# A two-layer hybrid attention encoder: its grouped attention written as 24 equal steps, the differential products scaled by GpSimd, one filler weight chunk converted a step sooner

## The chip, the cores and the metric

The kernel runs on one core of a Trainium2 chip. The metric is the device time of one execution in microseconds (us); the time before is 1885.14 us, the median of three runs (1883.15 to 1885.39).

## What is computed

Two sequences (256 and 512 tokens of width 1024) go through two layers and a final norm. A layer, from the reference:

```python
q_g, k_g, v_g, q_d, k_d, v_d = jnp.split(rms_norm(x) @ w_in, SPLITS, axis=-1)
o_g = softmax(q_g @ k_g.T * scale) @ v_g                                   # 8 heads of 64, 2 key/value heads
o_d = rms_norm((softmax(q1 @ k1.T) - lam * softmax(q2 @ k2.T)) @ v_d)      # 4 heads, values of 128
x = x + concat([o_g, o_d]) @ w_out
x = x + (silu(gate) * up) @ w_down
```

(These lines are the reference's, shortened.) Attention is over the whole sequence, without a mask. All arithmetic is 32-bit; the kernel splits each matmul operand into a rounded high part and a low part and adds three products (`mm3`, line 1676).

## The kernel before

Tokens stand in six tiles of 128 rows: t = 0, 1 belong to the short sequence ("prompt" tiles below, 256 keys) and t = 2 to 5 to the long one ("sample" tiles, 512 keys). A layer is the input projections, then attention, then the output projection and the feed-forward part. Only attention is touched. It has eight *pairs* p of two heads; p = 0 to 3 are grouped attention, p = 4 to 7 differential attention (one pair is one differential head with its two maps). Pair and tile give the step e = 6p + t, from 0 to 47; GROUPED is 24.

Each engine has its own instruction list, and the order of the work is that of these lists, written out by hand; semaphores (`Signal`) couple them. There is no planner. The work of a grouped step:

- TensorE (PE): `scores` of a head (three matmuls of 64 rows into one PSUM bank; four banks, 2·(t mod 2) + h), `transpose_prob` of its exponentials (2 or 4 blocks of 128), `product` with the values (10 or 20 matmuls of 64 columns).
- VectorE (DVE): `row_max` of a head's scores (line 1342), the low part of the transposed probabilities (`probT_low`, line 1368), reciprocals (`inverse_sums`, line 1349), `take_product` (line 1388), which scales the product into the `mix` tile.
- ScalarE (ACT): `exp` (line 925), the high part of the transposed probabilities (`probT_high`, line 946).

When the tiles of a pair are done, their `mix` blocks are transposed in two parts (t = 0, 1 and t = 2 to 5; `transpose_mix`, line 1746), and ACT and DVE split the result (`mixT_high`, line 940; `mixT_low`, line 1376). Once in a pair ACT and GpSimd (POOL) split the next pair's queries and keys (`split_high`, line 934; `split_low`, line 655), in a prompt and a sample part.

The grouped pair before (three functions `gqa_pair`, lines 955, 1401 and 1792) is not the same in all its six steps. TensorE asks for the scores of t = 3 with the two heads one behind the other, and so for those of t = 2; for t = 4, 5, 0 and 1 it puts a transpose or a product between the heads:

```python
scores(l, e0 + (T + 1), 1, 0)          # end of a pair, lines 1818 to 1823
gqa_product(l, p, t, 0, vcol)
scores(l, e0 + (T + 1), 1, 1)
gqa_product(l, p, t, 1, vcol)
scores(l, e0 + (T + 2), 2, 0, p * 2 + 3)
scores(l, e0 + (T + 2), 2, 1)
```

ScalarE's exponentials run up to two steps ahead. In pairs 1 and 2 one 128x1024 weight chunk of the output projection is converted at t = 3 (`high_at`, line 732, on ACT, and `low`, line 1119, on DVE).

The differential step (`diff_step`, lines 988, 1431 and 1861) has on TensorE: scores of both heads of step e + 2, a `fill` (six 128x512 matmuls of the output projection for pairs 0 to 3, line 1839), the transposes of the combined map, and the product of step e - 1. ScalarE reads each product twice from PSUM: `squares` (line 975) for its norm, and, after GpSimd has worked out the inverse root (`head_rms`, line 664), `normed` (line 982), which scales the product into `mix`. TensorE's next product waits for `normed` (signal `mix_diff`, line 1835). The fills need four chunks; the third and fourth are converted by ACT at the end of step 35 and by DVE at the ends of steps 35 and 36. In pair 7 ACT and DVE also convert four 128x512 operands (`output_high`, line 739; `operand_low`, line 1166). A mix transpose of a differential pair waits also for the low part of the step before, because it borrows that bank (line 1752). The first fill (e = 24) waits for the mix of pair 3 (line 1849), every later one for `add_fill` of the one before (lines 1476 and 1847).

## Time and profile before

| | |
|---|---|
| median of three runs | 1885.14 us |
| the profiled execution | 1883.45 us |
| its span, first to last instruction | 1881.6 us |
| TensorE busy, share of the span | 1788.8 us, 95% |
| VectorE busy | 1186.2 us, 63% |
| ScalarE busy | 824.1 us, 44% |
| GpSimd busy | 208.4 us, 11% |
| mean granted TensorE clock | 0.994 |
| differential stage of layer 0 | 285.7 to 384.3 us |

All steps below are made against the profiled execution; what it has outside its span is 1.85 us. The two layers run alike: in layer 1 the grouped and the differential stage stand about 925 us later. Matmuls are pipelined: the profile's end of one lies behind the start of the next, so the time that a matmul costs is read from start to start.

### The profile page before, as it was taken

Reading aid. Unit: us, or ns where it says so; the run is one execution under the profiler, and the core shown is the slowest. Engines: PE = TensorE matmul, PEld = TensorE weight load, DVE = VectorE, ACT = ScalarE, POOL = GpSimd, SP = SyncE. Lnnn points to the kernel's source line nnn. Section 1 sums busy time; section 2 is a strip of 40 time slices with the busy share of each in tenths; the row PEclk is TensorE's granted clock in tenths of the full one; section 3 lists DMA queues with packets and bytes.
Section 4 is the critical chain, followed back from the end, with each engine's and each line's share of the span. In section 5 each row is a group of like instructions: output and inputs, shape, how many; then the busy total and the mean of one; then the engine's idle time right before and its main releaser. Section 6 shows DMA issues by size and latency. Waiting matters only on the chain.

```text
span 1881.6 us, 28640 instructions
## 1 busy us (share of the span) xinstructions
PE 1788.8 (95%) x11280; PEld 1565.5 (83%) x11280; DVE 1186.2 (63%) x2055; ACT 824.1 (44%) x1807; POOL 208.4 (11%) x311
## 2 busy tenths in 40 slices
PE   5999899898999999999999999999989999999998
PEld 5888677677999999999888877677779898989896
DVE  4655777866656565656565467776757565756564
ACT  3323777744343433333332347676443342424242
POOL 2301123222000000000012011232400000000000
PEclk9999999999999999999999999999999999999999
DMA  4221000111231312121221110002022222222222
GB/s 155 68 68 45 13 13 1 36 56 56 68 90 46 90 45 90 45 90 45 68 68 57 56 34 13 13 24 68 1 79 68 68 68 68 68 68 68 68 74 84
DMA packets 121908, 108.20 MB, mean 58 GB/s; under 512 B 3472, under 2 KB 95760, under 8 KB 121776
## 3 DMA queue, kind: packets, MB, share of 16 engines
q1 hardware_dynamic: 120096, 100.74, 18.0%
q0 software_dynamic: 960, 3.28, 0.5%
q8 instruction: 90, 1.47, 0.3%
q10 hardware_dynamic: 720, 2.36, 0.3%
q14 instruction: 42, 0.34, 0.1%
HBM read 103.22 MB, written 3.15 MB: 57 GB/s over the span
## 4 chain that ended last, share of the span: by engine, by line
PE 83%; DVE 7%; ACT 6%; issue 2%; POOL 1%; DMA 1%; SPq 0%; POOLq 0%; ACTq 0%; DVEq 0%
PE bank L1678 15%; PE bank L1680 13%; PE bank L1679 13%; PE bank L2018 11%; PE bank L2022 11%; PE bank L2020 11%; PE bank L1768 3%; PE bank L1759 2%; ACT stage L931 2%; DVE neg_max L1346 1%; ACT stage L951 1%; DVE stage L1372 1%; PE bank L1937 1%; PE bank L1719 1%; POOL hrstd L607 1%
## 5 line engine op out<-in xcount | busy, mean ns | idle before, releaser
L1678 PE MATMUL bank<-w_hi,hT_hi 128*128 128x512 f32 (+1 forms) x624 | 244.7, 392 | 10.8 <-DVE w_lo L1121 4.6
L1680 PE MATMUL bank<-w_hi,hT_lo 128*128 128x512 f32 (+1 forms) x624 | 234.1, 375 | 0.0
L1679 PE MATMUL bank<-w_lo,hT_hi 128*128 128x512 f32 (+1 forms) x624 | 233.6, 374 | 0.0
L1242 DVE TENSOR_TENSOR x<-x,bank 128x512 f32<-128x512 f32 x120 | 81.2, 686 | 119.5 <-PE bank L1680 119.0
L1678 PEld LDWEIGHTS bank<-w_hi,hT_hi 128*128 128x128 f32 x624 | 117.9, 189 | 41.0 <-issue 8.5
L2018 PE MATMUL bank<-hT_hi,w_hi 128*128 128x384 f32 x368 | 125.3, 340 | 11.3 <-issue 7.4
L1680 PEld LDWEIGHTS bank<-w_hi,hT_lo 128*128 128x128 f32 x624 | 117.8, 189 | 21.6
L1768 PEld LDWEIGHTS bank<-v,stage 128*128 128x128 f16 x2400 | 102.0, 98 | 39.5 <-issue 25.3
L1679 PEld LDWEIGHTS bank<-w_lo,hT_hi 128*128 128x128 f32 x624 | 118.2, 189 | 17.2
L1768 PE MATMUL bank<-v,stage 128*128 128x64 bf16 (+1 forms) x2400 | 116.6, 203 | 13.2 <-DVE stage L1372 11.1
L2022 PE MATMUL bank<-hT_hi,w_lo 128*128 128x384 f32 x368 | 125.1, 340 | 0.0
L605 POOL TENSOR_TENSOR ms<-ss,eps_col 128x1 f32<-128x1 f32 x30 | 6.6, 220 | 1066.9 <-ACT headsq L779 1066.9
L2020 PE MATMUL bank<-hT_lo,w_hi 128*128 128x384 f32 x368 | 124.6, 339 | 0.0
L1121 DVE TENSOR_TENSOR w_lo<-w_raw,w_hi 128x1024 fp32r<-128x1024 f32 x48 | 58.7, 1223 | 103.8 <-ACT w_hi L730 103.6
L931 ACT ACTIVATE stage<-bank,neg_max 128x512 f32<-128x512 f32 (+1 forms) x192 | 117.1, 614 | 16.0 <-DVE neg_max L1346 15.4
L1346 DVE TENSOR_REDUCE neg_max<-bank 128x1 f32<-128x512 f32 (+1 forms) x192 | 111.3, 590 | 10.9 <-PE bank L1680 10.9
L760 ACT ACTIVATE w_hi<-w_raw 128x512 fp32r<-128x512 f32 x112 | 69.3, 624 | 93.9 <-DMA w_raw<-in_w_down_dram 32.9
L1678 PE MATMUL bank<-w_hi,actT_hi 128*128 128x512 f32 x264 | 104.6, 396 | 0.0
L1680 PE MATMUL bank<-w_hi,actT_lo 128*128 128x512 f32 x264 | 104.3, 395 | 0.0
L1679 PE MATMUL bank<-w_lo,actT_hi 128*128 128x512 f32 x264 | 104.2, 395 | 0.0
L730 ACT ACTIVATE w_hi<-w_raw 128x1024 fp32r<-128x1024 f32 x48 | 50.5, 1057 | 109.7 <-PE bank L1680 108.2
L1171 DVE TENSOR_TENSOR w_lo<-w_raw,w_hi 128x512 fp32r<-128x512 f32 x112 | 75.9, 694 | 22.5 <-ACT w_hi L760 22.5
(209 smaller groups left out, 4620.3 us busy)
## 6 DMA issues: line engine op xcount, KB each, us to landing
x_raw<-in_w_gate_up_dram SPq DMA_DIRECT2D x44, 512.0 KB, 5.1
w_raw<-in_w_gate_up_dram SPq DMA_DIRECT2D x44, 512.0 KB, 4.0
w_raw<-in_w_in_dram SPq DMA_DIRECT2D x36, 512.0 KB, 3.7
w_raw<-in_w_down_dram SPq DMA_DIRECT2D x36, 512.0 KB, 3.8
w_raw<-in_w_out_dram SPq DMA_DIRECT2D x16, 512.0 KB, 3.7
x_raw<-in_w_down_dram SPq DMA_DIRECT2D x8, 512.0 KB, 4.1
out_dram<-stage SPq DMA_DIRECT2D x6, 512.0 KB, 2.6
gain<-in_gains_dram POOLq DMA_DIRECT2D x5, 512.0 KB, 4.8
```

The lines of the kernel that those rows point to most:

```text
L760: act.activation(ring_of(r)[0], raw_of(s)[:, off:off + COLS], ACT.Copy).then_inc(ff_hi.sem, 1)
L931: act.activation(prob[:, b, h, 0:S], bank[:, 2 * b + h, 0:S], ACT.Exp, bias=neg_max[:, b, h:h + 1], accum_out=row_sum[:, t, h:h + 1]).then ...
L1171: dve.tensor_tensor(lo, raw_of(s)[:, off:off + COLS], hi.bitcast(F32), ALU.subtract).then_inc(ff_lo.sem, 1)
L1242: dve.tensor_tensor(xs, xs, bank[:, DOWN_BANK[t], :], ALU.add).then_inc(x_added.sem, 1)
L1346: dve.tensor_reduce(neg_max[:, b, h:h + 1], bank[:, 2 * b + h, 0:S], AX.X, ALU.max, negate=True).then_inc(max_done.sem, 1)
L1678: pe.matmul(out, a_hi, b_hi, start=first, stop=False)
L1679: pe.matmul(out, a_hi, b_lo, start=False, stop=False)
L1680: return pe.matmul(out, a_lo, b_hi, start=False, stop=last)
L1768: last = pe.matmul(out, probT[:, b, a, k, :], v[i][:, k0 // P + k, at(vcol, width)], start=(k, a, i) == terms[0], stop=(k, a, i) == terms[-1])
L2018: pe.matmul(o, b_hi[:, cols], a_hi[:, k, :], start=begin, stop=False, skip_group_check=True)
L2020: pe.matmul(o, b_hi[:, cols], a_lo[:, k, :], start=False, stop=False, skip_group_check=True)
L2022: last = pe.matmul(o, b_lo[:, cols], a_hi[:, k, :], start=False, stop=end, skip_group_check=True)
```

## The change

Grouped attention becomes 24 calls of one `grouped_step` on each engine. TensorE asks for the scores of both heads of step e + 2 together, behind the first head's transposes; the product of a step's second head moves into the next step. `row_max` reduces both heads (two PSUM banks) in one instruction, in the differential steps too, and both heads' exponentials wait for that one signal. ScalarE's exponentials are now one step ahead, and the mix parts are transposed at t = 3 of their own pair and t = 1 of the next (for pair 3 at step 24, inside the first differential step). `normed` goes: ScalarE copies the product unscaled into `mix` right behind `squares` (signal `o_taken`), and GpSimd multiplies it there by the inverse root. The third filler chunk is converted by ACT at the end of step 34 and by DVE at the beginning of step 35; the fourth by ACT at the end of step 35, as before, and by DVE at the beginning of step 36. The diff, without declarations of unchanged meaning:

```diff
 def mixed_at(e):
     p, t = divmod(e, 6)
-    return (p, 0) if t == 4 else (p - 1, 1) if t == 2 and p > PAIRS // 2 else None
+    if e < GROUPED:
+        return (p, 0) if t == 3 else (p - 1, 1) if t == 1 and p else None
+    return (PAIRS // 2 - 1, 1) if e == GROUPED else (p, 0) if t == 4 else (p - 1, 1) if t == 2 and p > PAIRS // 2 else None
...
+        o_taken = Signal("o_taken", 4 * T, credit=1)
+        mix_diff = Signal("mix_diff", 4 * T)
...
                 c = slice(t, t + 1)
                 inverse_rms(l, (p - 4) * T + t, oss[:, c], oss_done, oms[:, c], oms_done, orstd[:, c], orstd_done,
                             eps_row[:, c])
+                pool.wait_ge(orstd_done.sem, orstd_done.at(l, (p - 4) * T + t))
+                pool.wait_ge(o_taken.sem, o_taken.at(l, (p - 4) * T + t))
+                pool.tensor_scalar(mix[:, t, :], mix[:, t, :], orstd[:, c], None, ALU.mult).then_inc(mix_diff.sem, 1)
...
-                act.wait_ge(max_done.sem, max_done.at(l, e * 2 + h))
+                act.wait_ge(max_done.sem, max_done.at(l, e))
                 act.activation(prob[:, b, h, 0:S], bank[:, 2 * b + h, 0:S], ACT.Exp, bias=neg_max[:, b, h:h + 1],
                                accum_out=row_sum[:, t, h:h + 1]).then_inc(exp_done.sem, 1)
...
-            def gqa_pair(l, p, following):
-                e0 = p * T
-                for t in range(T):
-                    probT_high(l, e0 + t, t, 0, 0, P_SCALE)
-                    if t:
-                        exp(l, e0 + (t + 1), (t + 1) % T, 1)
-                    probT_high(l, e0 + t, t, 1, 1, P_SCALE)
-                    exp(l, e0 + (t + 2), (t + 2) % T, 0)
-                    if t == 2:
-                        mixT_high(l, p, 0, True)
-                    if t in (2, 4):
-                        split_high(t // 2 - 1, q_hi, following[0])
-                        split_high(t // 2 - 1, k_hi, following[1])
-                    if t == 3 and p in (1, 2):
-                        high_at(l, CHUNKS_IN + p - 1)
-                exp(l, e0 + (T + 1), 1, 1)
-                mixT_high(l, p, 1, True)
+            def grouped_step(l, e):
+                p, t = divmod(e, T)
+                probT_high(l, e, t, 0, 0, P_SCALE)
+                if mixed_at(e):
+                    mixT_high(l, *mixed_at(e), True)
+                for h in range(2):
+                    exp(l, e + 1, (t + 1) % T, h)
+                probT_high(l, e, t, 1, 1, P_SCALE)
+                if t in (1, 4):
+                    split_high(t // 4, q_hi, p + 1)
+                    split_high(t // 4, k_hi, 8 + (p + 1) // 2 if p < 3 else 10)
+                if t == 3 and p in (1, 2):
+                    high_at(l, CHUNKS_IN + p - 1)
...
-            def normed(l, p, t):
-                act.wait_ge(orstd_done.sem, orstd_done.at(l, (p - 4) * T + t))
-                act.activation(mix[:, t, :], bank[:, BANK_O, 0:P], ACT.Copy,
-                               scale=orstd[:, t:t + 1]).then_inc(mix_diff.sem, 1)
+                act.activation(mix[:, t, :], bank[:, BANK_O, 0:P], ACT.Copy).then_inc(o_taken.sem, 1)
...
-                if e >= GROUPED + 2:
-                    normed(l, *divmod(e - 2, T))
                 if mixed_at(e):
-                    mixT_high(l, *mixed_at(e), False, e)
+                    mixT_high(l, *mixed_at(e), e == GROUPED, e)
...
-                if e == 5 * T + 5:
-                    high_at(l, CHUNKS_IN + 2)
-                    high_at(l, CHUNKS_IN + 3)
+                if e in (5 * T + 4, 5 * T + 5):
+                    high_at(l, CHUNKS_IN + e - 5 * T - 2)
...
+                for h in range(2):
+                    exp(l, 0, 0, h)
+                for e in range(GROUPED):
+                    grouped_step(l, e)
+                for h in range(2):
+                    exp(l, GROUPED + 1, 1, h)
...
-            def row_max(l, e, t, h):
+            def row_max(l, e, t):
                 S = seq_of(t)[1]
                 b = t % 2
-                dve.wait_ge(scores_done.sem, scores_done.at(l, e * 2 + h))
-                dve.tensor_reduce(neg_max[:, b, h:h + 1], bank[:, 2 * b + h, 0:S], AX.X, ALU.max,
+                dve.wait_ge(scores_done.sem, scores_done.at(l, e * 2 + 1))
+                dve.tensor_reduce(neg_max[:, b, :], bank[:, 2 * b:2 * b + 2, 0:S], AX.X, ALU.max,
                                   negate=True).then_inc(max_done.sem, 1)
...
-            def gqa_pair(l, p):
-                e0 = p * T
-                for t in range(T):
-                    if t >= 3:
-                        row_max(l, e0 + (t + 1), (t + 1) % T, 1)
-                    probT_low(l, e0 + t, t, 0, 0, P_SCALE)
-                    inverse_sums(l, e0 + t, t)
-                    if t >= 2 and t < T - 1:
-                        row_max(l, e0 + (t + 2), (t + 2) % T, 0)
-                    if t:
-                        take_product(l, e0 + (t - 1), t - 1)
-                    probT_low(l, e0 + t, t, 1, 1, P_SCALE)
-                    if t == 0:
-                        for h in range(2):
-                            row_max(l, e0 + 3, 3, h)
-                    if t == 2:
-                        mixT_low(l, p, 0, True)
-                    if t == 3 and p in (1, 2):
-                        low(l, CHUNKS_IN + p - 1, CHUNKS_IN + p - 1)
-                for h in range(2):
-                    row_max(l, e0 + (T + 1), 1, h)
-                take_product(l, e0 + (T - 1), T - 1)
-                next_maxima(l, e0 + (T + 2))
-                mixT_low(l, p, 1, True)
+            def grouped_step(l, e):
+                p, t = divmod(e, T)
+                if e:
+                    probT_low(l, e - 1, (t - 1) % T, 1, 1, P_SCALE)
+                probT_low(l, e, t, 0, 0, P_SCALE)
+                if mixed_at(e):
+                    mixT_low(l, *mixed_at(e), True)
+                row_max(l, e + 2, (t + 2) % T)
+                inverse_sums(l, e, t)
+                if e:
+                    take_product(l, e - 1, (t - 1) % T)
+                if t == 3 and p in (1, 2):
+                    low(l, CHUNKS_IN + p - 1, CHUNKS_IN + p - 1)
...
-                ahead = GROUPED < e < STEPS - 2
+                if e in (5 * T + 5, 6 * T):
+                    n = CHUNKS_IN + (2 if e < 6 * T else 3)
+                    low(l, n, n)
                 if combining:
                     inverse_sums(l, e + 1, (t + 1) % T)
-                if ahead:
-                    row_max(l, e + 2, (t + 2) % T, 0)
-                if combining:
                     map_ratio(l, *divmod(e + 1, T))
-                if ahead:
-                    row_max(l, e + 2, (t + 2) % T, 1)
+                if e + 2 < STEPS:
+                    row_max(l, e + 2, (t + 2) % T)
                 if combining:
                     combine(l, *divmod(e + 1, T))
                 if mixed_at(e):
-                    mixT_low(l, *mixed_at(e), False, e)
+                    mixT_low(l, *mixed_at(e), e == GROUPED, e)
                 probT_low(l, e, t, 0, t % 2, map_scale[:, :])
                 if t % 2:
                     add_fill(l, (e - GROUPED) // 2)
-                if e in (5 * T + 5, 6 * T):
-                    n = CHUNKS_IN + (2 if e < 6 * T else 3)
-                    low(l, n, n)
...
+                for e in range(GROUPED):
+                    grouped_step(l, e)
+                probT_low(l, GROUPED - 1, T - 1, 1, 1, P_SCALE)
+                take_product(l, GROUPED - 1, T - 1)
                 second_map_in(l, 4, 0)
...
-            def scores(l, e, t, h, split=None, first=False):
+            def scores(l, e, split=None):
+                t = e % T
                 k0, S, _ = seq_of(t)
                 b = t % 2
                 if split is not None:
                     pe.wait_ge(qk_split.sem, qk_split.at(l, split * 2 + 1))
-                if not first:
-                    pe.wait_ge(exp_done.sem, exp_done.at(l, (e - 2) * 2 + h))
-                rows = slice(h * HD, (h + 1) * HD)
-                mm3(bank[:, 2 * b + h, 0:S], q_hi[rows, t * P:(t + 1) * P], q_lo[rows, t * P:(t + 1) * P],
-                    k_hi[rows, k0:k0 + S], k_lo[rows, k0:k0 + S], True, True).then_inc(scores_done.sem, 1)
+                if e >= 2:
+                    pe.wait_ge(exp_done.sem, exp_done.at(l, (e - 2) * 2 + 1))
+                for h in range(2):
+                    rows = slice(h * HD, (h + 1) * HD)
+                    mm3(bank[:, 2 * b + h, 0:S], q_hi[rows, t * P:(t + 1) * P], q_lo[rows, t * P:(t + 1) * P],
+                        k_hi[rows, k0:k0 + S], k_lo[rows, k0:k0 + S], True, True).then_inc(scores_done.sem, 1)
...
-                e = p * T + t
+            def grouped_product(l, e, h):
+                p, t = divmod(e, T)
                 if h == 0:
                     pe.wait_ge(mix_gqa.sem, mix_gqa.at(l, e - 2))
-                    bank_free_of_mix(l, p, t)
+                    if mixed_at(e):
+                        q, part = mixed_at(e)
+                        pe.wait_ge(mixT_lo_done.sem, mixT_lo_done.at(l, 2 * q + part))
                 pe.wait_ge(pT_lo[h].sem, pT_lo[h].at(l, e))
-                last = product(t, bank[:, BANK_O + t % 2, h * HD:(h + 1) * HD], h, vcol, HD)
+                last = product(t, bank[:, BANK_O + t % 2, h * HD:(h + 1) * HD], h, p // 2 * HD, HD)
                 if h:
                     last.then_inc(o_done.sem, 1)
...
+            def grouped_step(l, e):
+                p, t = divmod(e, T)
                 gqa_transpose(l, e, t, 0)
-                gqa_product(l, p, T - 2, 1, vcol)
+                if mixed_at(e):
+                    transpose_mix(l, *mixed_at(e), True)
+                scores(l, e + 2, {4: p * 2 + 2, 0: p * 2 + 1}.get(t))
+                if e:
+                    grouped_product(l, e - 1, 1)
                 gqa_transpose(l, e, t, 1)
-                scores(l, e0 + (T + 1), 1, 0)
-                gqa_product(l, p, t, 0, vcol)
-                scores(l, e0 + (T + 1), 1, 1)
-                gqa_product(l, p, t, 1, vcol)
-                scores(l, e0 + (T + 2), 2, 0, p * 2 + 3)
-                scores(l, e0 + (T + 2), 2, 1)
-                transpose_mix(l, p, 1, True)
+                grouped_product(l, e, 0)
...
-                pe.wait_ge(mix_diff.sem, mix_diff.at(l, e - GROUPED - 1))
+                pe.wait_ge(o_taken.sem, o_taken.at(l, e - GROUPED - 1))
                 pe.wait_ge(pT_lo[0].sem, pT_lo[0].at(l, e))
                 product(t, bank[:, BANK_O, 0:P], t % 2, (p - 3) * P, P).then_inc(o_done.sem, 1)
...
-                if GROUPED < e < STEPS - 2:
-                    for h in range(2):
-                        scores(l, e + 2, (t + 2) % T, h, {4: p * 2 + 2, 0: p * 2 + 1}.get(t) if h == 0 else None)
+                if e < STEPS - 2:
+                    scores(l, e + 2, {4: p * 2 + 2, 0: p * 2 + 1}.get(t))
                 if mixed_at(e):
-                    transpose_mix(l, *mixed_at(e), False, e)
+                    transpose_mix(l, *mixed_at(e), e == GROUPED, e)
                 fill(l, e - GROUPED)
-                if mixed_at(e - 1):
+                if e > GROUPED and mixed_at(e - 1):
                     q, part = mixed_at(e - 1)
                     pe.wait_ge(mixT_lo_done.sem, mixT_lo_done.at(l, 2 * q + part))
...
+                for t in range(2):
+                    pe.wait_ge(v_rest.sem, v_rest.at(l, T + 2 * t + 1))
+                    scores(l, t, None if t else 0)
+                pe.wait_ge(v_rest.sem, v_rest.at(l, 2 * T - 1))
+                pe.wait_ge(qkT_done.sem, qkT_done.at(l, 4 * T - 1))
+                for e in range(GROUPED):
+                    grouped_step(l, e)
+                grouped_product(l, GROUPED - 1, 1)
```

`grouped_step` calls functions that stand as before (`probT_high`, `exp`, `probT_low`, `inverse_sums`, `take_product`, `gqa_transpose`, `transpose_mix`).

## Rows read from the trace of the kernel before

**Rows 1.** Windows: stretch, length, busy us of PE, PEld, DVE, ACT, POOL, granted clock.
```profile
217.63:240.11 22.48, 20.35 (x284) 15.33 (x283) 17.06 (x40) 16.60 (x43) 3.91 (x4) 1.00 0.08 25
...
285.70:384.28 98.58, 92.08 (x782) 72.72 (x783) 76.11 (x164) 73.60 (x231) 31.19 (x58) 1.00 0.12 33
...
193.30:199.80 6.50, 6.50 (x40) 4.51 (x40) 3.95 (x9) 3.35 (x12) 0.00 (x0) 0.50 0.00 0
```
**Rows 2.** Waits, whole run: engine, line, releaser: us in total, times, longest.
```profile
PE bank L1768 <- DVE stage L1372: 11.1, 24, 0.7
```
**Rows 3.** Timeline of PE, one grouped pair of layer 0: start, us, instruction.
```profile
193.29 1.16 PE L1678 MATMUL bank<-k_hi,q_hi 64*128 64x512 f32 x2 [3.04 <-ACT stage L931]
...
216.24 0.51 PE L1678 MATMUL bank<-k_hi,q_hi 64*128 64x512 f32 x2
...
217.14 0.66 PE L1754 MATMUL bank<-ident,mix 128*128 128x128 f32 x4
217.63 0.60 PE L1759 MATMUL bank<-ident,stage 128*128 128x128 f32 x4
...
223.29 0.47 PE L1768 MATMUL bank<-v,stage 128*128 128x64 bf16 x10
223.59 0.64 PE L1759 MATMUL bank<-ident,stage 128*128 128x128 f32 x4
224.16 0.50 PE L1678 MATMUL bank<-k_hi,q_hi 64*128 64x512 f32 x1
...
225.04 0.76 PE L1768 MATMUL bank<-v,stage 128*128 128x64 bf16 x20
...
230.54 0.38 PE L1678 MATMUL bank<-k_hi,q_hi 64*128 64x256 f32 x1
...
231.09 0.76 PE L1768 MATMUL bank<-v,stage 128*128 128x64 bf16 x20
```
**Rows 4.** Groups by form, 217.63 to 240.11: names, shapes, count, busy us, mean ns, idle.
```profile
L1346 DVE TENSOR_REDUCE neg_max<-bank 128x1 f32<-128x512 f32 x9 | 6.0, 680 | 1.2 <-PE bank L1680 1.2
L1372 DVE SCALAR_TENSOR_TENSOR stage<-bank,stage 128x512 f16<-128x512 f32 x8 | 5.5, 690 | 2.4 <-ACT stage L951 2.1
L931 ACT ACTIVATE stage<-bank,neg_max 128x512 f32<-128x512 f32 x8 | 5.5, 688 | 1.4 <-DVE neg_max L1346 1.4
L951 ACT ACTIVATE stage<-bank 128x512 f16<-128x512 f32 x8 | 4.8, 596 | 0.9 <-PE bank L1759 0.7
...
L1346 DVE TENSOR_REDUCE neg_max<-bank 128x1 f32<-128x256 f32 x4 | 1.7, 414 | 0.2 <-PE bank L1680 0.2
...
L1121 DVE TENSOR_TENSOR w_lo<-w_raw,w_hi 128x1024 fp32r<-128x1024 f32 x1 | 1.2, 1225 | 0.9 <-ACT w_hi L730 0.9
```
**Rows 5.** Timeline of PE where the grouped stage of layer 0 ends.
```profile
283.56 0.66 PE L1754 MATMUL bank<-ident,mix 128*128 128x128 f32 x4
285.73 0.47 PE L1678 MATMUL bank<-w_hi,hT_hi 128*128 128x512 f32 x1 [1.50 <-DVE hT_lo L1382]
```
**Rows 6.** Waits of PE, 285 to 400: line, releaser, us in total, times, longest.
```profile
PE bank L1678 <- DVE w_lo L1121: 2.3, 2, 2.1
PE bank L1754 <- DVE stage L1372: 2.1, 2, 1.5
...
PE bank L1768 <- ACT mix L985: 0.8, 4, 0.2
```
**Rows 7.** Groups by form of GpSimd and one copy, 285.7 to 383, layer 0.
```profile
L985 ACT ACTIVATE mix<-bank,orstd 128x128 f32<-128x128 f32 x23 | 8.5, 368 | 9.5 <-POOL orstd L607 9.1
...
L660 POOL TENSOR_TENSOR k_lo<-qkT,k_hi 128x256 fp32r<-128x256 f32 x3 | 3.7, 1223 | 0.0
...
L660 POOL TENSOR_TENSOR q_lo<-qkT,q_hi 128x256 fp32r<-128x256 f32 x3 | 2.2, 748 | 0.0
```
**Rows 8.** Timeline, all engines, where the differential stage of layer 0 ends.
```profile
385.22 0.55 POOL L607 TENSOR_TENSOR orstd<-oms,neg_half 128x1 f32<-128x1 f32 x1
...
387.16 0.60 PE L1754 MATMUL bank<-ident,mix 128*128 128x128 f32 x4
```

53 lines of the change are left out of this document (4 added, 49 removed).

## The prediction, made before the changed kernel was run

> **What bounds the kernel now.** I read the windows of the attention stage first, then TensorE's waits, then its timeline. TensorE sets the pace: a grouped pair lasts 22.48 us, TensorE is busy for 20.35 of them, VectorE 17.06, ScalarE 16.60; the differential stage has 92.08 busy of 98.58 [rows 1]. What is left between is waiting: products of grouped steps wait for the low part of their probabilities, 24 times, 11.1 us in both layers [rows 2]. The rows to look at are the scores. Where both heads are asked for together, the next work starts 0.90 us later (216.24 to 217.14); where one head stands alone, it takes 0.88 (224.16 to 225.04) [rows 3]. The second head of a pair of calls is thus nearly free, and the old order pays in full for it at t = 4, 5, 0 and 1.
>
> **Scores asked for together.** For a sample tile 2 x 0.88 becomes 0.90: 0.86 saved, twice in a pair. For a prompt tile one head takes 0.55 (230.54 to 231.09) [rows 3]; both together are shown in no row here, so they lie between 0.55 and 1.10; I take 0.57, by the sample row: 0.53 saved, twice in a pair. That is 2.78 a pair and **11.1 us a layer** of TensorE's work; with the prompt tile's upper bound it would be 6.9.
>
> **The waits of the new grouped order.** I worked through the three lists with start-to-start times from the rows: four transposes 0.57, paired scores 0.90, a product of 20 matmuls 0.60 (twice the 0.30 of ten) [rows 3]; high part 0.60, exponential 0.69 (with its accumulator read 0.78 to the end), low part 0.69, each with the next instruction of its engine starting some 0.1 before the end [rows 4]. A sample step is 3.2 us of TensorE, 2.4 of ScalarE and 2.7 of VectorE, so TensorE stays the longest. The maximum over two banks is not in the trace. From 0.41 for 256 columns and 0.68 for 512 the slope gives 1.22 for 1024, and a subtraction of 1024 columns takes 1.225 [rows 4]; the ends are 1.22 and twice 0.68 = 1.36 if it saves nothing, more in a rival below. I take 1.22. In a pair four things end late:
> - t = 1: the mix transposes wait for `take_product` of t = 5, which stands behind a two-bank maximum in VectorE's list: 0.4.
> - t = 2: the low parts of both heads come late because ScalarE does the two prompt splits first: 0.2.
> - t = 3: the mix transposes again, for `take_product` of t = 1: 0.3.
> - t = 5: the first product waits while ScalarE does two sample splits ahead of its high part: 0.5.
>
> Pair 0 lacks the first: 5.2 a layer. In pairs 1 and 2 a chunk is converted at t = 3. Before, a maximum stood behind it on VectorE; now the low part of t = 3's second head does, and TensorE waits for that. From the end of those transposes: high part 0.60, ScalarE's chunk 1.06 (estimate: the 0.60 of 512 columns, doubled, less the fixed share), VectorE's 1.22, low part 0.69, some 0.2 of signals: 3.75, against 1.75 that TensorE has to do (a product, four transposes, prompt scores). It waits 2.0, twice: 4.0 a layer; the ends are 0.5 (the wait that such a place shows now [rows 2]) and 2.0. At the end of the stage the last product has nothing to hide its low part: 0.95. At the seam the first fill starts 2.17 after the mix transposes now, 1.68 beyond their own 0.49 [rows 3, 5]; the new list puts a combine and one-column instructions ahead of `mixT_low`, some 0.9 (estimate from 0.41 for 256 columns, and as much again): 2.6. Sum: 5.2 + 4.0 + 0.95 + 2.6 = **12.75**.
>
> The same measure before: 12 waits of 0.46 [rows 2], each 0.17 longer from start to start (a product at 223.29 with 0.47 on the page is followed at 223.59 [rows 3]), 7.6, and the seam's 1.68: **9.3**. So waits grow by 3.45 and the grouped stage gets 11.1 - 3.45 = **7.65 us a layer** shorter. The stage's start gives nothing: TensorE idles 3.04 us there for exponentials that wait for VectorE's work on the values, and then runs 6.5 us at a granted clock of 0.50, that is 1.2 of 2.4 GHz [rows 1, 3]; the same work is to be done in it.
>
> **The differential steps.** ScalarE's instructions stay as many: a raw copy for a scaled one of the same shape, 0.37 [rows 7]. What goes is its wait for GpSimd, 9.1 us in a stage [rows 7], of which only 0.8 reached TensorE [rows 6]; I count 0.6, since one of the four waits stands just ahead of a longer one. The copy now stands ahead of `output_high` in pair 7, and VectorE waits for that: the two mix waits, 2.1 [rows 6], grow by 0.27 each, with the two-bank order by 0.3: +0.6. GpSimd's scaling, 24 a layer, is not in the trace: between a one-column operation (0.55 [rows 8]) and 256 columns with two inputs (0.75 [rows 7]). I take 0.6. Queued behind it are only the next head's inverse root and the query and key splits, which are read a step or more later; what waits for it, the mix transposes, comes two steps later, and at the stage's end there are 1.39 us between the end of the inverse root and these transposes (385.77 to 387.16 [rows 8]): nothing on the path. If that cover went, 0.6 a layer. The merged maximum lets the first exponential of a step wait 0.54 longer (1.22 against 0.68 [rows 4]); in ScalarE's list it stands behind the high part of the step's map, and that behind a fill on TensorE, so nothing ends later.
>
> Against this stands a rule. GpSimd's split of 256 columns takes 0.75 in one place and 1.22 in another, where VectorE combines maps beside it [rows 7]; the mean shows the slowing, and VectorE's side is small. The Trainium skill (SBUF — State Buffer, "SBUF: two separate sides") makes it an exclusive lock: a GpSimd operation and a VectorE operation with two SBUF inputs block each other for a whole instruction. By that rule every one of the 24 scalings could hold a combine up; it would reach the path at the three places where VectorE ends last, 3 x 0.6 a layer, and the sum would be 3.6 us less gain.
>
> The third chunk: the fill of step 36 waits 2.1 and that of step 37 0.2 for chunks [rows 6]. With the chunk a step earlier, `add_fill` of step 35 ends last in its place: behind the chunk (1.22) VectorE has the maximum, a combine, a low part and that add. Worked through, step 36 still waits 1.2 and step 37 not at all: **1.0 to 1.3 gained**, the ends 0 and 2.3. SP's next chunk load is released by the same conversion, so it comes earlier; that chunk is used only after step 47.
>
> The stage sums to -1.3 - 0.6 + 0.6 = **-1.3 a layer**. Both layers: 2 x (7.65 + 1.3) = 17.9. The profiled execution took 1883.45, the median is 1.69 above it: 1885.1 - 17.9 = **1867**.
>
> **Rivals.**
> - *The clock falls at the new waits.* An idle of 3.04 us was followed by a clock of 0.50 for 6.5 us, one of 2.1 at step 36 by none [rows 1, 3, 6]. The seam's 2.6 lies between them, the chunk waits at 2.0. Each fall costs half of 6.5, 3.25: the seams alone give 1873.5, the four chunk waits as well 1886. The Trainium skill (TensorE: Matmul & The Clock Gate, Part 1) has the same rule, that an idle stretch halves the clock until work has been sustained. Chance 0.13.
> - *The waits are shorter.* If the chunk conversion is hidden as it is now, 1859. Chance 0.1.
> - *Waits take everything back.* With exponentials one step ahead instead of two, each late signal reaches TensorE; a third of a us more in each of the 48 grouped steps would do it: about 1883. For it: every engine has 70% or more to do; against it: the worked lists. Chance 0.06.
> - *The change does not do what it says:* prompt or sample scores do not overlap behind transposes. All 22 us stay unsaved: 1889. The paired calls at 216.24 speak against it. Chance 0.04.
> - *Slower: the two-bank maximum.* If crossing a bank made it cost double, 2.44, VectorE's pair would grow by 4 x 1.22 + 2 x 0.68 = 6.2 to 23.3, above the old 22.48, and the differential stage's 72.72 by over 20 to some 95 of 98.6, with in-order waits on top: some 8 us a layer, 1900. It decides from about 1.9 us on. No instruction of before reads two banks, so only the slope speaks against it. Chance 0.07.
>
> **The numbers.** The forecast has 0.6 and a range of its own of 1861 to 1873 (prompt pairing, chunk, seam). For 8 in 10 the range takes in the shorter waits and the clock at the seams: 1857 to 1877. A measurement of this kernel tells some 0.2% from no change, 3.8 us. Faster by more: 0.6 + 0.1 + 0.11 of the clock case + 0.03 of full waits = 0.84; within: 0.08; slower: 0.08.
>
> **What would show it.** Both heads' score matmuls merged at every step, a pair without a chunk at 18 to 19 us and one with a chunk at 20 to 20.5; `row_max` at 1.2 us; the wait before products at t = 4 of pairs 1 and 2 at 2 us; the seam above 2 us; no PE wait for `mix` on ScalarE; the chunk wait at step 36 replaced by one for `add_fill`. Pairs above 21 us, maxima above 1.4 us or a granted clock below 1 after the start would make it wrong.

## The result, and the profile after

The changed kernel takes **1867.01 us** (median of 4 runs, 1862.12 to 1870.84) where the kernel before takes 1885.27 (4 runs beside it): ratio 0.9901, 95% interval 0.9879 to 0.9923, that is 18.3 us faster with some 4 us of uncertainty. The forecast was 1867, 17.9 faster. The sum came out; this section and the next show that not all of its terms did.

The profiled execution took 1870.84 us, the slowest of the four, with a mean granted clock of 0.987 (before: 0.994). Windows of it: stretch, length, busy time of PE, PEld, DVE, ACT, POOL, granted clock, and last the DMA share and GB/s. The first is the start of grouped attention, the second and third are pairs 1 and 2, each from the second block of transposes of its step t = 1 to that of the next pair's, and the last three are stretches right behind a wait.

```profile
193.06:199.80 6.74, 6.74 (x50) 4.47 (x51) 3.66 (x7) 3.82 (x14) 0.00 (x0) 0.51 0.00 0
214.71:234.66 19.95, 17.51 (x288) 13.50 (x285) 16.29 (x34) 16.35 (x44) 3.94 (x4) 1.00 0.10 28
234.66:255.76 21.10, 18.92 (x288) 15.08 (x285) 16.42 (x34) 16.55 (x44) 3.95 (x4) 0.92 0.08 26
247.38:251.00 3.62, 3.62 (x48) 3.55 (x48) 2.20 (x5) 1.43 (x3) 0.23 (x1) 0.53 0.43 149
276.78:280.50 3.72, 3.72 (x15) 2.25 (x15) 0.48 (x1) 1.49 (x4) 0.00 (x0) 0.68 0.00 0
365.99:369.50 3.51, 3.42 (x11) 2.57 (x12) 2.59 (x6) 1.51 (x7) 1.64 (x3) 0.62 0.14 27
```

A pair that lasted 22.48 [rows 1] lasts 19.95. Pair 2 does the same work in 21.10: in it a stretch runs at 0.53 of the clock. The start is as it was [rows 1].

The timeline of PE, at a prompt tile's scores, pair 0's t = 5, pair 1 from t = 1 to t = 4, the two chunk waits, the seam (the end of the grouped stage), and three waits of the differential stage (start, duration, instruction, idle time before and its releaser):

```profile
206.82 0.39 PE L1652 MATMUL bank<-k_hi,q_hi 64*128 64x256 f32 x2
...
207.38 0.29 PE L1744 MATMUL bank<-v,stage 128*128 128x64 bf16 x4
...
210.74 0.63 PE L1735 MATMUL bank<-ident,stage 128*128 128x128 f32 x4
211.75 0.74 PE L1744 MATMUL bank<-v,stage 128*128 128x64 bf16 x20 [0.37 <-DVE stage L1364]
...
215.27 0.66 PE L1730 MATMUL bank<-ident,mix 128*128 128x128 f32 x4
...
218.24 0.51 PE L1652 MATMUL bank<-k_hi,q_hi 64*128 64x512 f32 x2
...
219.14 0.32 PE L1744 MATMUL bank<-v,stage 128*128 128x64 bf16 x5
...
219.45 0.64 PE L1735 MATMUL bank<-ident,stage 128*128 128x128 f32 x4
220.14 0.74 PE L1744 MATMUL bank<-v,stage 128*128 128x64 bf16 x20
220.72 0.63 PE L1735 MATMUL bank<-ident,stage 128*128 128x128 f32 x4
221.44 0.44 PE L1730 MATMUL bank<-ident,mix 128*128 128x128 f32 x2
...
223.31 0.63 PE L1735 MATMUL bank<-ident,stage 128*128 128x128 f32 x4
223.78 0.75 PE L1744 MATMUL bank<-v,stage 128*128 128x64 bf16 x20
...
227.44 0.76 PE L1744 MATMUL bank<-v,stage 128*128 128x64 bf16 x20 [1.89 <-DVE stage L1364]
...
247.38 1.25 PE L1744 MATMUL bank<-v,stage 128*128 128x64 bf16 x20 [1.89 <-DVE stage L1364]
...
272.25 0.76 PE L1744 MATMUL bank<-v,stage 128*128 128x64 bf16 x20 [0.62 <-DVE stage L1364]
...
273.84 0.65 PE L1730 MATMUL bank<-ident,mix 128*128 128x128 f32 x4
276.78 0.47 PE L1652 MATMUL bank<-w_hi,hT_hi 128*128 128x512 f32 x1 [2.29 <-DVE hT_lo L1374]
...
324.53 0.47 PE L1652 MATMUL bank<-w_hi,hT_hi 128*128 128x512 f32 x1 [1.28 <-DVE x L1453]
...
332.25 0.63 PE L1730 MATMUL bank<-ident,mix 128*128 128x128 f32 x4 [0.59 <-DVE stage L1364]
...
365.99 0.41 PE L1730 MATMUL bank<-ident,mix 128*128 128x128 f32 x2 [2.30 <-DVE stage L1364]
```

Both heads' scores are merged (x2) at every step and cost 0.56 (206.82 to 207.38) and 0.90 (218.24 to 219.14) together; a single head cost 0.55 and 0.88 [rows 3]. From the first work after the start's wait to the first fill it is 83.72 us (193.06 to 276.78), before 92.44 (193.29 to 285.73, [rows 3, 5]): the grouped stage is **8.7 us** shorter in this execution, and 9.0 in the other layer (1111.07 to 1194.52, before 1118.24 to 1210.64).

The waits of PE from 185 to 400 us (engine, line, releaser: us in total, times, longest):

```profile
PE bank L1744 <- DVE stage L1364: 5.4, 6, 1.9
PE bank L1730 <- DVE stage L1364: 3.8, 3, 2.3
...
PE bank L1652 <- DVE hT_lo L1374: 2.3, 1, 2.3
```

Grouped products wait six times, 5.4 us (before, 24 times 11.1 in both layers, 5.55 a layer [rows 2]). No wait for ScalarE's copy is left (0.8 before [rows 6]), and the filler waits for the sum into x (1.28 at 324.53) where it waited 2.1 for `w_lo` [rows 6]. But the mix transposes of the differential stage wait 3.8 where they waited 2.1 [rows 6].

Groups of the differential stage, 276.78 to 375 (names, shapes, count, busy, mean ns, idle):

```profile
L1338 DVE TENSOR_REDUCE neg_max<-bank 128x2 f32<-128x1024 f32 x15 | 18.2, 1217 | 0.0
L672 POOL TENSOR_SCALAR mix<-mix,orstd 128x128 f32<-128x128 f32 x22 | 16.2, 735 | 2.2
```

The maximum over two banks takes 1.22 us. GpSimd's scaling takes 0.74 in the mean. The raw copy takes 0.28 (shown in run 7); the scaled one took 0.37 [rows 7].

### The profile page after: what moved, and what is told of

Read it like the earlier page. It is cut to its first block, busy times and chain, and to the rows that moved or that the text cites. A ratio compares the mean times of both kernels' runs of the same rounds, so it can differ in the third digit from the quotient of the medians.

```text
span 1868.8 us, 28636 instructions
## 1 busy us (share of the span) xinstructions
PE 1776.8 (95%) x11280; PEld 1560.3 (83%) x11280; DVE 1181.0 (63%) x1959; ACT 815.9 (44%) x1807; POOL 240.4 (13%) x359
## 4 chain that ended last, share of the span: by engine, by line
PE 80%; DVE 10%; ACT 6%; issue 2%; DMA 1%; POOL 1%; SPq 0%; POOLq 0%; ACTq 0%; DVEq 0%
PE bank L1652 14%; PE bank L1654 13%; PE bank L1653 13%; PE bank L1968 11%; PE bank L1972 11%; PE bank L1970 11%; DVE neg_max L1338 2%; ACT stage L937 2%; PE bank L1744 2%; PE bank L1735 2%; ACT stage L957 1%; DVE stage L1364 1%; PE bank L1887 1%; PE bank L1693 1%; DVE w_lo L1113 1%
## 5 line engine op out<-in xcount | busy, mean ns | idle before, releaser
L1744 PEld LDWEIGHTS bank<-v,stage 128*128 128x128 f16 x2400 | 106.5, 100 | 29.8 <-DVE stage L1364 13.5
L1338 DVE TENSOR_REDUCE neg_max<-bank 128x2 f32<-128x1024 f32 (+1 forms) x96 | 99.5, 1038 | 3.1 <-PE bank L1654 2.4
L1735 PE MATMUL bank<-ident,stage 128*128 128x128 f32 x480 | 83.6, 291 | 6.6 <-ACT stage L937 6.6
```

Source lines behind the costliest of these rows:

```text
L1338: dve.tensor_reduce(neg_max[:, b, :], bank[:, 2 * b:2 * b + 2, 0:S], AX.X, ALU.max, negate=True).then_inc(max_done.sem, 1)
L1735: last = pe.transpose(bank[:, BANK_PT + b, k * P:(k + 1) * P], prob[:, t % 2, h, k * P:(k + 1) * P], ident[:, :])
L1744: last = pe.matmul(out, probT[:, b, a, k, :], v[i][:, k0 // P + k, at(vcol, width)], start=(k, a, i) == terms[0], stop=(k, a, i) == terms[-1])
```

## The experiments

Each was timed beside the kernel before; I compare ratios to it. Each ratio has an interval of plus or minus 0.13 to 0.25%, 2.5 to 4.6 us, and the difference of two of them is less certain than either, by some 4 to 5 us. Of smaller differences only the traces speak. `e_same`, the changed kernel once more, gives the yardstick.

> The changed kernel once more, unchanged, to have it on the same chip as the two beside it and to see how far its runs differ with the granted clock: 1867 by both theories, between 1862 and 1871, the lower ones with the higher mean clock.

Measured: 1865.1 us (4 runs, 1864.42 to 1867.32), ratio 0.9902 (0.9886 to 0.9918), as in the first timing. Its profiled run had a clock of 0.989 and took 1867.32; of the first timing's runs the fastest, 1862.12, had 0.994. The spread of the changed kernel goes with the clock.

**1. The scores of the two heads apart.**

```diff
-                scores(l, e + 2, ...)
-                if e:
-                    grouped_product(l, e - 1, 1)
+                for h in range(2):
+                    head_scores(l, e + 2, h, ...)
+                    if h == 0 and e:
+                        grouped_product(l, e - 1, 1)
```

> The changed kernel with the scores of the two heads pulled apart again on TensorE: head 0's three matmuls, the product of the step before, then head 1's three. Nothing else moves. Theory (TensorE's own work sets the length of a grouped step): a sample step's scores take 0.88 + 0.88 us instead of 0.90 and a prompt step's 0.55 + 0.55 instead of 0.56, so 2.8 to 4.5 us a pair, 11 to 14 a layer with the last steps' unmoved, 22 to 28 us in all: 1889 to 1895. Rival (the steps wait for VectorE and ScalarE, the pairing is hidden in their round): head 1's scores come later by one product (0.75 us), so the maximum does too, but TensorE's time falls into waits that are there anyway: under 8 us in all. A second rival: the longer matmul time closes the short waits, the clock stays up, and the cost is between the two, 10 to 18.

Measured: 1916.68 us, ratio 1.0168 (1.0145 to 1.0191): **49.7 us** more than the changed kernel, by far the largest effect. It is more than the whole gain, since the kernel before had asked for some of the heads together. The expectation had an error of its own: four sample steps at 0.88 and two prompt steps at 0.55 are 4.6 us a pair, not 2.8 to 4.5 (the forecast's 2.78 counts only the steps that were apart before). Pair 1 by its window, and part of pair 1 in the timeline:

```profile
217.95:244.44 26.49, 23.93 (x289) 18.02 (x285) 16.69 (x34) 16.73 (x44) 3.92 (x4) 0.94 0.07 21
```

```profile
238.19 0.38 PE L1652 MATMUL bank<-k_hi,q_hi 64*128 64x256 f32 x1
...
238.74 0.76 PE L1756 MATMUL bank<-v,stage 128*128 128x64 bf16 x20
239.43 0.38 PE L1652 MATMUL bank<-k_hi,q_hi 64*128 64x256 f32 x1
...
245.52 0.66 PE L1742 MATMUL bank<-ident,mix 128*128 128x128 f32 x4 [0.66 <-DVE mix L1383]
```

Pair 1 is 6.5 us longer than in the changed kernel (26.49 at a clock of 0.94, 19.95 at 1.00). A single head takes 0.55 here too (238.19 to 238.74); a product followed by scores takes 0.69 to the next start (238.74 to 239.43), one followed by transposes 0.58 (220.14 to 220.72 in the changed kernel). So 4.6 + 6 x 0.1 = 5.2 of work a pair, and a new wait of 0.66 for the mix (at 245.52, in pair 2): 5.9, 47 us in all. None of it fell into waits: TensorE sets the length of the grouped steps, and the rival of hidden scores is out.

**2. The chunk's low part one step later.**

```diff
-                if t == 3 and p in (1, 2):
+                if t == 4 and p in (1, 2):
                     low(l, CHUNKS_IN + p - 1, CHUNKS_IN + p - 1)
```

> The changed kernel with VectorE's low part of the filler chunk in pairs 1 and 2 moved one step later, from the end of step 3 to the end of step 4; ScalarE's half stays where it is. Theory: the 1.89 us that the products wait in each of these pairs is VectorE standing in line for ScalarE's chunk copy and then taking 1.2 us for its own part, with the low parts of the transposed map queued behind it. One step later the copy is long done, VectorE does not stand, and the wait falls to about 0.8 us (the 1.2 us of work less the slack of some 0.4): 2 x 1.1 a layer, 4 to 5 us in all, and another 2 to 3 us a layer of low clock may go where the clock fell after this wait: 1859 to 1863 against the changed kernel's 1867. Rival: the 1.2 us of VectorE's work is what costs, wherever it stands, and the wait only moves to the next step: 1866 to 1868.

Measured: 1860.64 us, ratio 0.9873 (0.9852 to 0.9894), some 5 us faster than the changed kernel (0.0028 of 1885), about as much as the two intervals can tell apart. The wait in pair 1:

```profile
225.49 0.74 PE L1744 MATMUL bank<-v,stage 128*128 128x64 bf16 x20 [0.17 <-DVE stage L1364]
...
227.99 0.76 PE L1744 MATMUL bank<-v,stage 128*128 128x64 bf16 x20 [0.72 <-DVE stage L1364]
```

The 1.89 became 0.17 and 0.72. Why, the changed kernel's VectorE shows:

```profile
225.55 1.23 DVE L1113 TENSOR_TENSOR w_lo<-w_raw,w_hi 128x1024 fp32r<-128x1024 f32 x1 [1.12 <-ACT w_hi L736]
226.70 1.28 DVE L1364 SCALAR_TENSOR_TENSOR stage<-bank,stage 128x512 f16<-128x512 f32 x2
```

VectorE stood 1.12 us for ScalarE's half of the chunk, and the low part that the product needed stood behind it. As expected.

**3. The seam's low part first.**

```diff
+                if e == GROUPED:
+                    mixT_low(l, *mixed_at(e), True, e)
                 if e + 2 < STEPS:
                     row_max(l, e + 2, (t + 2) % T)
```

> The changed kernel with VectorE's low part of the last grouped mix (what the first filler step waits for) put ahead of the row maximum and the combination in the first differential step. Theory: the 2.29 us that the filler waits at the seam are ScalarE's high part (0.6) and then the row maximum of 1.22 and the combination of 0.74 in which VectorE is caught; without them the low part starts when the high part ends, and the wait falls to 1.0 to 1.3 us: 1.0 to 1.3 a layer, 2 to 2.6 us in all, and up to 1.7 us a layer more where the clock fell after the wait: 1862 to 1865. Rival: the maximum then comes 1.2 to 1.5 us later, the exponentials and the first differential product with it, and the wait comes back at the next step: 1866 to 1869.

Measured: 1865.27 us, ratio 0.9894 (0.9874 to 0.9915); by time alone no difference from the changed kernel. The wait fell from 2.29 to 1.50, less than expected:

```profile
272.79 0.69 DVE L1374 TENSOR_TENSOR hT_lo<-bank,hT_hi 128x512 fp32r<-128x512 f32 x1 [0.65 <-ACT hT_hi L949]
```

Now VectorE waits for ScalarE there; what is left is the chain transposes, high part, low part, as before [rows 5].

**4. Maxima per head in the differential steps.**

```diff
                     inverse_sums(l, e + 1, (t + 1) % T)
+                    head_max(l, e + 2, (t + 2) % T, 0)
                     map_ratio(l, *divmod(e + 1, T))
-                    row_max(l, e + 2, (t + 2) % T)
+                    head_max(l, e + 2, (t + 2) % T, 1)
```

> The changed kernel with the maxima of the differential steps taken per head again, as in the kernel before (0.68 + 0.68 us instead of 1.22 over both banks, head 0's right behind the reciprocal, its exponential released at once); the grouped steps keep the merged maximum. Theory: the merged maximum is what made the last pair's mix transposes wait 2.30 us instead of 1.47, and 0.59 and 0.91 at the two before, since head 0's exponential waits for both heads' maxima and the squares and the copy stand behind it on ScalarE. Per head these waits go back by 0.5 to 1.0 each in the last pair, 1 to 2 us a layer, 2 to 4 in all: 1863 to 1865. Rival: the tail is late because the copy now stands ahead of the output's high part on ScalarE, and the maxima cost only their sum on VectorE, 0.14 us a step in slack: 1867 to 1869 with the same waits.

Measured: 1866.49 us, ratio 0.9899 (0.9877 to 0.9921): no difference. The mix transposes' waits in layer 0:

```profile
PE bank L1740 <- DVE stage L1371: 2.8, 2, 2.0
```

1.0 less than in the changed kernel. Of that, 0.59 is the wait in pair 6 (332.25 in the changed kernel), which is gone; the two waits of the last pair fell only from 3.2 to 2.8. The expectation had counted all three to the last pair. So the maximum has a small share in the tail, and the longest wait is still 2.0: the rest has another cause.

**5. ScalarE scales the product again.**

```diff
-                pool.tensor_scalar(mix[:, t, :], mix[:, t, :], orstd[:, c], None, ALU.mult).then_inc(mix_diff.sem, 1)
...
+                if e >= GROUPED + 2:
+                    normed(l, *divmod(e - 2, T))
```

> The changed kernel with the differential product scaled by ScalarE again as it is copied (the scaled copy waits for GpSimd's inverse norm and stands at the head of the next step but one), and nothing scaled by GpSimd; the grouped steps and the chunk stay as changed. Theory (by the prediction's terms: the waits of the scaled copy cost 0.6 us a layer, and the raw copy ahead of the output's high part costs 0.6): the two cancel, 1865 to 1869, and the last pair's mix waits (2.30, 0.91, 0.59 us) fall by some 0.5 in all. Rival: the 9.1 us a layer that ScalarE stood waiting for GpSimd come back on the path of the products and the low parts: 4 to 8 us in all, 1871 to 1875. Second rival: raw copy and GpSimd's scaling are what makes the tail late, and without them it is 1 to 2 us a layer faster: 1863 to 1865.

Measured: 1866.5 us, ratio 0.9902 (0.9887 to 0.9917): the two cancel. The waits:

```profile
PE bank L1735 <- DVE stage L1369: 2.3, 2, 1.5
...
PE bank L1749 <- ACT mix L982: 1.5, 5, 0.6
```

The mix transposes wait 1.5 less, the products 1.5 more, for ScalarE's copy. GpSimd's scaling by itself brought nothing.

**6. The third chunk as before.**

```diff
-                if e in (5 * T + 4, 5 * T + 5):
-                    high_at(l, CHUNKS_IN + e - 5 * T - 2)
+                if e == 5 * T + 5:
+                    high_at(l, CHUNKS_IN + 2)
+                    high_at(l, CHUNKS_IN + 3)
```

(and VectorE's `low` back behind `add_fill`.)

> The changed kernel with the third filler chunk converted as in the kernel before: ScalarE's two halves of it and the fourth both in the last step of pair 5, VectorE's low parts at the end of their steps instead of the front. Theory: the filler that opens the second block waits again for the low part, 2.1 us, where it waits 1.28 for the sum into x now: 1.0 to 1.3 a layer, 2 to 2.6 in all: 1869 to 1870, and 1 to 2 more a layer if the clock falls after a wait of that length. Rival: the wait for the sum and the wait for the low part end together, and nothing is seen: 1866 to 1868.

Measured: 1870.85 us, ratio 0.9920 (0.9906 to 0.9934), some 3 to 4 us slower than the changed kernel; the intervals overlap, so the time alone does not show it.

```profile
324.83 0.61 PE L1653 MATMUL bank<-w_hi,hT_hi 128*128 128x512 f32 x1 [2.37 <-DVE w_lo L1114]
```

2.37 for `w_lo` where the changed kernel waits 1.28 for x: the theory's 1.1 a layer. Behind this wait the granted clock was 0.54 for 3.67 us (324.83 to 328.50), behind the 1.28 it was 1.00.

**7. The output's high part first.**

```diff
                 probT_high(l, e, t, 0, t % 2, map_scale[:, :])
+                if p == PAIRS - 1 and t < OUT_R:
+                    output_high(l, t)
                 if e + 2 < STEPS:
                     for h in range(2):
                         exp(l, e + 2, (t + 2) % T, h)
```

> The changed kernel with ScalarE's high part of the output weights (last pair, four steps) moved ahead of the step's two exponentials and of the squares and the copy. Theory (the last pair's steps run in a round: VectorE's maximum, ScalarE's two exponentials, squares, copy, output high part, then VectorE's output low part, which stands at the head of the next step's reciprocal and maximum): with the high part out of the round VectorE does not stand 0.5 us a step for it, and ScalarE fills time in which it waited 0.7 to 1.3 us for the maximum; the mix transposes' wait of 2.30 us falls by 1 to 2, and with it the low clock behind it: 1 to 2.5 us a layer, 1862 to 1865. Rival: the round is bound by VectorE's own work (1.22 + 0.74 + 0.74 + 0.74 + 0.69 and the small ones, 4.6 us a step) and only 0.2 to 0.4 a step is won, hidden in TensorE's waits for other things: 1866 to 1868.

Measured: 1862.01 us, ratio 0.9877 (0.9863 to 0.9891), about 4.5 us faster than the changed kernel.

```profile
PE bank L1730 <- DVE stage L1364: 1.6, 2, 1.0
```

The mix transposes wait 1.6 instead of 3.8. The round that it cut stands in the changed kernel's VectorE and ScalarE, first VectorE:

```profile
362.37 0.69 DVE L1163 TENSOR_TENSOR ring_lo<-w_raw,ring_hi 128x512 fp32r<-128x512 f32 x1 [0.48 <-ACT ring_hi L749]
...
363.31 1.22 DVE L1338 TENSOR_REDUCE neg_max<-bank 128x2 f32<-128x1024 f32 x1
```

```profile
361.54 0.28 ACT L982 ACTIVATE mix<-bank 128x128 f32<-128x128 f32 x1
361.69 0.65 ACT L749 ACTIVATE ring_hi<-w_raw 128x512 fp32r<-128x512 f32 x1
...
364.56 0.69 ACT L937 ACTIVATE stage<-bank,neg_max 128x512 f32<-128x512 f32 x1 [1.26 <-DVE neg_max L1338]
```

VectorE's maximum stands behind its output low part, that waits for ScalarE's output high part, which stands behind the copy and the exponentials, and these wait for the last maximum.

**8. The three together** (edits 2, 3 and 7).

> The changed kernel with three edits together: the low part of the chunk of pairs 1 and 2 one step later (6.4 us by its own run), the low part of the last grouped mix ahead of the maximum at the seam (1.7 us), the output's high part ahead of the exponentials in the last pair (2 to 5 us by its theory). Theory: the three stand at three places of the layer and add up: 10 to 13 us, 1854 to 1857, with a mean clock of 0.993 or more since the longest waits go. Rival: the clock's falls only move to the waits that are left (the first scores' 3.3 us, the filler's 1.3), and the gain is 6 to 8: 1859 to 1861.

Measured: **1852.71 us** (1849.94 to 1854.12), ratio **0.9828** (0.9815 to 0.9841): faster than both kernels, 32 us (1.7%) below the kernel before and 14 below the changed one. The parts add up: 5 and 1 and 4.5 by their own runs, and some 3 more. The waits of 1.89, 2.29 and 2.30 are down to 0.73, 1.50 and 1.05. The mean granted clock was 0.992 to 0.996 in its four runs, 0.987 to 0.994 in the changed kernel's; a run of each at 0.994 took 1853 and 1862, 9 us apart. So a part of the 14 us may be the clock. That it stays up because the waits are shorter is likely, but not shown: `e_same` with the old waits had 1.00 from 300 to 400 us too.

**9. Grouped steps alone** (new grouped steps; edits 4, 5 and 6 together put the differential stage back).

> The new grouped steps with the differential part put back as it was: maxima per head, the product scaled by ScalarE, the third chunk converted late. Theory (the prediction's terms): the grouped steps are worth 7.65 us a layer, 15.3 in all, 1869 to 1871, and the three parts of the differential stage the rest, of which the third chunk alone is worth 4 by its run and the other two nothing. Rival: the maxima and the scaling cancel each other only as long as the other one is there (both stand on the last pair's round), and with both put back the tail is shorter by 1 to 2 us a layer: 1865 to 1868.

Measured: 1866.14 us, ratio 0.9906 (0.9889 to 0.9922): as fast as the changed kernel, within the uncertainty. The time lies in the rival's range, though the interval does not exclude the theory's 1869. The trace decides: the grouped stage alone is 8.8 us shorter than before in one layer and 9.9 in the other (193.70 to 277.35, 1112.61 to 1195.10), together 18.7, the whole gain of 18.4. The three edits of the differential stage sum to nothing that can be measured. Its waits of PE from 270 to 400:

```profile
PE bank L1668 <- DVE w_lo L1119: 2.3, 2, 2.1
...
PE bank L1746 <- DVE stage L1377: 2.1, 2, 1.5
...
PE bank L1668 <- DVE x L1469: 0.9, 1, 0.9
PE bank L1760 <- ACT mix L982: 0.8, 4, 0.2
```

6.1 us in the differential stage; the changed kernel's `e_same` run has 3.8 and 2.2 there, 6.0. What the third chunk and the copy gave, the tail took.

**10. The chunk on GpSimd** (edits 3 and 7, and `low` of pairs 1 and 2 issued by GpSimd behind its second split).

> The version with the seam's low part first and the output's high part first, and the chunk's low part of pairs 1 and 2 given to GpSimd, behind its own low parts of the next pair's second half, so that VectorE has no chunk in the grouped steps at all. Theory: the two waits of 0.73 and 0.17 us in pairs 1 and 2 that are left with the chunk one step later (1852.7 us) fall to the 0.37 of pairs 0 and 3: 0.5 a pair, 1 a layer, 2 in all: 1850 to 1851. Rival: GpSimd takes 3 to 5 us for it (its 128 x 256 subtractions take 0.75 to 1.22 now), and VectorE's instructions beside it get longer, as they did beside GpSimd's scaling, or the next pair's low parts come late: 1853 to 1858.

Measured: 1852.91 us, ratio 0.9838 (0.9820 to 0.9856): the same as with edit 2.

```profile
L668 POOL TENSOR_TENSOR w_lo<-w_raw,w_hi 128x1024 fp32r<-128x1024 f32 x2 | 4.8, 2375 | 0.0
```

```profile
PE bank L1751 <- DVE stage L1371: 2.5, 7, 0.6
```

GpSimd takes 2.4 us, less than the rival said, and the products' waits fell from 3.2 to 2.5 a layer, 1.4 in all, less than the times can show; the clock of this profiled run was 0.991 against 0.996.

**11. The three together, ScalarE scaling** (edits 2, 3, 7 and 5).

> The version with the three edits (chunk one step later, the seam's low part first, the output's high part first: 1852.7 us) with the differential product scaled by ScalarE again, as in the kernel before. Theory (the changed kernel with ScalarE's scaling is as fast as with GpSimd's, 1866.5 against 1867, and the tail's round is now cut): the same, 1851 to 1855. Rival: with the output's high part ahead of the exponentials ScalarE is the engine that the last pair's round waits for, and its wait for GpSimd's norm at the head of each step comes on top, 0.2 to 0.8 a step in the last pair and where the product waits for the copy: 2 to 5 us slower, 1855 to 1858.

Measured: 1854.68 us, ratio 0.9852 (0.9827 to 0.9876). The interval reaches over that of run 8: no difference shown, with or without GpSimd's scaling. Products wait 2.4 us a layer for ScalarE's copy, the mix transposes hardly at all; again the one replaces the other.

## Why the forecast came out, point by point

- **Scores asked for together: right, and worth more than counted.** 0.90 and 0.56 instead of twice 0.88 and 0.55, in every step. By the Trainium skill (TensorE: Matmul & The Clock Gate, Part 3) small matmuls can run side by side in one array; the trace agrees, the second head costs 0.01 to 0.02 us. That they lie on the path, run 1 shows: each us of them is a us of the kernel. What the forecast left out is the instruction ahead of a head's scores: four transposes cost 0.57 before scores (223.59 to 224.16 [rows 3]) and 0.47 before a product (223.31 to 223.78), a product 0.69 and 0.58. A pair had ten blocks of scores and now has six, so some 0.4 a pair comes on top: some 12.8 a layer instead of 11.1.
- **The waits of the new grouped order: right in their places, somewhat too high.** The forecast counted 12.75 us a layer from start to start, against 9.3 before. On the page the waits look smaller, 5.4 + 2.3, because it counts idle time from the modelled end of a matmul, which lies behind the next one's start. From start to start, four transposes are followed by a product after 0.47 where nothing is late. At t = 5 it takes 1.01 (210.74 to 211.75), late by 0.54, given as 0.5; at t = 2 0.69 (219.45 to 220.14), late by 0.2 as given; at t = 3 0.72 to the mix transposes (220.72 to 221.44), late by 0.25, given as 0.3; at t = 1 two transposes take 0.56 (214.71 to 215.27) instead of some 0.25, late by 0.3, given as 0.4. Not every pair has all four: some 4 to 4.5 a layer, given as 5.2. The chunk cost 1.95 twice (given as 2.0), the last product 0.8 (0.95), the seam 276.78 - 273.84 - 0.49 = 2.45 (2.6). That is some 11.5 to 12. The kernel before has 8.9 by the same measure. So the waits grew by some 3, given as 3.45, and the grouped steps are worth some 10 us a layer instead of 7.65. One layer of run 9 shows just that, 9.9.
- **The clock: a rival that came in part.** This execution got 8.7, not 9.9. In layer 0 its clock fell behind one of the two chunk waits (0.53 for 3.62 us), at the seam (0.68) and in the last pair (0.62). The fall inside the grouped stage made pair 2 1.15 us longer than pair 1 (21.10 against 19.95), which is the missing part within the uncertainty of this count. The one behind the wait of 2.30 cost 1.6: from 365.99 to the feed-forward part's first wait at 412.17 it is 46.18 us, in `e_same`, where a wait of 2.31 at that place was followed by 1.00, 44.58 (364.87 to 409.45). The rival had priced each at 3.25, half of a stretch of 6.5; the slow stretches lasted only 3.5 to 3.7 us, and waits behind them took up a part. The forecast had named a pair above 21 us and a clock below 1 after the start as signs against it. Both were seen; the sum held because the grouped steps gave more than it said.
- **The differential stage: the step that failed.** -1.3 a layer, 2.6 in all, became nothing (run 9). From the first fill to the feed-forward part's first wait it is 133.04 in `e_same`, where the clock stayed up (276.41 to 409.45), against 132.63 before (285.73 to 418.36): +0.4 a layer, and +2.8 in the profiled execution (135.39). The third chunk was right, 1.28 for x instead of 2.37 for `w_lo` (run 6). The copy's waits, 0.8 on the page, went, as said. But the tail, put at +0.6, came to +1.1 in the last pair (0.91 + 2.30 against 2.1 [rows 6]), and in pair 6 a wait of 0.59 is new. The argument that a first exponential that waits 0.54 longer lets "nothing end later" fails there: the exponentials, the copy, the output's high and low parts and the next maximum form a round, and the copy (run 5: 2.3 left of 3.8) and the merged maximum (run 4: 2.8 left) each lengthen it.
- **The two-bank maximum: right,** 1.22. The slower rival is out. Its estimate for the differential stage started from 72.72, which is the weight loads' column; VectorE's is 76.11 [rows 1].
- **GpSimd's scaling: right that nothing waits for it;** its size, 0.74 for 0.6, mattered nowhere. By the lock that the Trainium skill (SBUF — State Buffer, "SBUF: two separate sides") states, each scaling could hold up a combine. The trace agrees for GpSimd's side only: 16 of the 24 scalings of layer 0 took 0.61; the other eight took 0.87 to 1.37, and all of them had started while VectorE ran an operation with two SBUF inputs of 512 columns or more (0.91 at 293.44 beside a combine, 1.37 at 320.91 beside a chunk's low part). The combines of 512 columns beside scalings kept their 0.74, and no wait of TensorE is put down to GpSimd. The mean combine of 512 columns was 742 ns in the changed kernel, 783 in run 5 without scalings, 807 in the kernel before (300 to 345 us of each), and run 5 is no faster.

So the number was right partly by luck. The grouped steps gave some 2 us a layer more than forecast, and the differential stage and the clock's falls took about as much away. The sign and the mechanism (paired scores on a TensorE that sets the pace) were right for the reason given: run 1 takes the pairing back and loses more than the gain, run 9 keeps only the grouped steps and has all of it.

Open: no run kept the clock from falling while leaving the waits, so why it falls behind one wait and not behind another of the same length stays open. Single edits (runs 2 to 7) and the variants 10 and 11 are told apart by their waits more than by their times; runs 2 and 7 stand at the margin of what the times can show, the others below it.

## What to carry to other kernels

Where one engine sets the pace, its saved work is worth its full length, less what its waits grow. Count waits from start to start, before and after alike: a wait of 0.2 us does not appear on the page where the end of one matmul overlaps the next (t = 2 and t = 3 here). Count also what an instruction costs in front of the one that is merged away. The long waits came from a few places where an engine stands in line for another with the needed work behind it. Look in the trace for exactly that pattern (an instruction that waits with the product's own input queued behind it); moving that one instruction was worth 4 to 6 us in two of three cases here (runs 2 and 7; run 3 less than the times can show), while moving work between ScalarE and GpSimd was worth nothing. A wait for A that goes away can come back as a wait for B at the same place, so judge a group of edits by undoing all of it at once, too.

## What the hardware did that I had not expected

- The granted clock fell behind waits shorter than I had thought. A wait of 1.89 us at 247.38 was followed by 0.53 for 3.62 us, the same wait of 1.89 at 227.44 by 1.00 (pair 1's window); one of 2.29 by 0.68, and one of 2.30 by 0.62. In the kernel before one of 2.1 was followed by none [rows 1, 6], in run 6 one of 2.37 at the same place by 0.54. A fall cost 1.15 us in pair 2 and 1.6 in the last pair. The same kernel's runs spread over 9 us, in the order of their mean clock (0.987: 1870.84, 0.994: 1862.12).
- A product costs 0.58 before transposes and 0.69 before a head's scores (220.14 to 220.72, and run 1): the change from 128 rows to 64 is not free.
- GpSimd subtracts 128 x 1024 in 2.4 us, about twice VectorE's 1.23, and VectorE's instructions beside it kept their length (its low parts of 512 columns took 690 ns in the mean with it, 689 without, from 215 to 256 us).
